# Moving the pieces of a later chunk's trunk between the gather steps of the chunk before it

## The chip, the cores and the metric

The kernel runs on one core of one Trainium2 chip. A time is the device's time for one execution, in microseconds (us); three runs of the kernel before gave a median of 3059.66 us (3058.35 to 3059.75). One further execution was recorded by the profiler, and all rows below are from it. The engines are TensorE (PE, matmuls, and PEld for its weight loads), VectorE (DVE), ScalarE (ACT), GpSimd (POOL) and SyncE (SP), which only asks for DMA transfers here.

## The reference

One layer of a decoder over 1024 prompt tokens and 8 sample tokens of width 1024, in float32:

```
h = rmsnorm(x);  u, x_lru, y_lru, g_a, g_b = split(h @ w_in)
a_out = S5(u): 32 groups, complex state of 64, h_t = a h_{t-1} + B u_t, y = C h + d u,
        z = gelu(y), a_out = z * sigmoid(z @ w_glu + b_glu)
b_out = RG-LRU(conv4(x_lru)) * gelu(y_lru):  r, i = sigmoid(block-diagonal gates of xc),
        log_a = -8 r softplus(-lam), h_t = exp(log_a) h_{t-1} + sqrt(1 - exp(2 log_a)) (i * xc)
x = x + (sigmoid(g_a) * (a_out @ w_proj_a) + sigmoid(g_b) * (b_out @ w_proj_b)) @ w_out
# PEER: 8 heads x top 16 of 128 x 128 experts a token
q = rmsnorm(x) @ w_q;  scores of two key halves, top 16 of each, top 16 of the 256 sums
x = x + sum over 128 experts e of  softmax(score)_e * gelu(u_tab[e] . x) * v_tab[e]
y = rmsnorm(x)
```

The outputs are y for both kinds of tokens and the last states of S5, RG-LRU and the convolution.

## The kernel before

**Chunks and steps.** The prompt is cut into CH = 4 chunks of C = 256 tokens. What stands ahead of PEER (in-projection, convolution, S5, RG-LRU, GLU, mixing, output, queries and lists of experts) is called a chunk's trunk. PEER then takes, for each of a chunk's two tiles of 128 tokens, 128 experts a token: one indirect DMA by POOL (`gather`, L802) brings for 128 tokens the row of u and the row of v of one expert each, 128 x 8 KB = 1.05 MB. There are 1032 of them in all. Two gathers are one step (PAIR = 2) and a chunk has BC = 128 steps. For each gather DVE does one dot product over 1024 elements (L1825, with a read-out of its sum), ACT weighs it (L856), and PE does eight matmuls on v (`values`, L2273, of the step before).

**What lets a gather go.** The u rows stand in a ring of CHAINS = 5, the v rows in a ring of UV = 10. POOL's gather i waits until the dot product of gather i-5 is done (`u_used`), and until the matmuls of gather i-10 are. So the order of work on DVE decides when POOL may ask for the next rows: a DVE that waits for something else holds the gathers.

**The calendar.** The trunk of chunk c (1 to 3) runs between the last steps of chunk c-1. Each engine has its own program, written out in order; before a piece of the trunk it calls `upto(t)`, which first lets the engine do its part of the gather steps up to calendar time t. A time t up to 96 is a step of chunk c-1: step 48 + 80t/96 (rounded down) for chunk 1, step 32 + t for chunks 2 and 3; from 96 on it is a step of the chunk itself. The functions `at_...` (from L126) give the times. Nothing but semaphores ties the engines to each other: where the calendars of a maker and of a user of data give the same step, the user waits for the maker with its own gather work still to do behind the wait.

**The pieces that the change touches.** On DVE a later chunk's list is `LATER_DVE`, "CCCC--" + "SSSS" + "LLS" four times + 16 "S": piece n stands at `at_piece(n)`. C is a convolution, L a piece of the RG-LRU recurrence (`lru`, L1315 and L1620; the first L of a chunk waits for `tanh_ok`, which ACT's square root gives), S a piece of S5 (`s5`, L1307, L1582), three to each of 8 pairs of state rows. The first piece of a pair waits for `bu_ok`: PE's `s5_in` (L2178, 16 matmuls of 32 x 128) at `at_s5_in(jp)`. The first `s5_in` also waits for ACT, which must have copied the inputs u out of PE's banks. Then come PE's gate units (`project`, L2161, at `at_ga`), the four GLU units (L2161; ACT; then DVE's L1315, four of 128 x 256), the eight mixing units (`mix`: L2317 on PE at `at_mix(m)`, three L1315 on DVE at `at_mix(m)` + 1) and the eight output units (`out`, L2337, at `at_out(k)`).

**Weights.** SP brings a pair of weight tiles of 1 MB (w_in, L678), or 512 KB (w_glu, w_ab), when the slot of an earlier pair comes free.

```
def at_s5_in(jp):
    return max(at_scan(PIECES * jp) - 2, 9)
def steps_at(c, t):
    old = BC - own(c - 1) if c else OLD
    return t * old // OLD if t <= OLD else old + t - OLD
```

Of the kernel before, what the change touches and what calls it, by code (L numbers as in the profile page):

```python
# [72 lines left out]
LAST_FIRST = (6, 7, 0, 1, 2, 3, 4, 5)  # L73


AT_GATE, AT_GA, AT_GLU, AT_MIX, AT_OUT, AT_X2, AT_TR, AT_PROJ, AT_Q = 8, 24, 51, 53, 62, 71, 74, 75, 81
SECOND_AT = 10

TRUNK_W = [("w_in", m) for m in range(28)] + [("w_glu", m) for m in range(4)]
# [44 lines left out]


def at_piece(n):  # L126
    return 3 + 6 * n // 5


def at_scan(k):  # L130

    return at_piece([n for n, kind in enumerate(LATER_DVE) if kind == "S"][k])
# [30 lines left out]

def at_ga(m):

    return AT_GA + 25 * m // 16


def later_u(q):
# [10 lines left out]


def at_mix(m):
    return AT_MIX + m


def at_out(k):
    return AT_OUT + 9 * k // 8


def at_proj(h, s):  # L190
# [201 lines left out]
def build(nc, i_, o_):  # L392

    with ExitStack() as ctx:
# [459 lines left out]
        def _(act):  # L854
# [224 lines left out]
            def chunk(c, last):  # L1079
# [95 lines left out]
                else:  # L1175
# [32 lines left out]
                    for m in range(2 * KT):  # L1208
                        z_until(at_ga(m) + 1)
                        upto(at_ga(m) + 1)  # L1210
                        mixing_gate(m)
# [91 lines left out]
        def _(dve):  # L1303
# [724 lines left out]
            def chunk(c, last):  # L2028
# [13 lines left out]
                for n_piece, kind in enumerate(FIRST_DVE if first else LATER_DVE):  # L2042
                    upto(at_piece(n_piece))
                    if kind == "S":
                        next(scans)
                    elif kind == "L":
                        next(gates)
                    elif kind == "C" and not first:
                        conv(c, convs, last)
                        convs += 1  # L2050
                        if convs == QT:
                            if last:
                                V.tensor_copy(hsmp, xl[:, :, 3 + C:3 + N])
                            V.tensor_copy(halo, xl[:, :, C:C + 3]).then_inc(halo_ok, 1)
# [9 lines left out]
                for m in range(KT):  # L2064
                    upto(at_mix(m) + 1)
                    mix(c, m, units(c) + U_MIX + m, slice(0, n), MIXB[m % 2])
# [59 lines left out]
        def _(pe):  # L2126
# [348 lines left out]
            def chunk(c, last):  # L2475
# [48 lines left out]
                else:  # L2524
# [12 lines left out]
                    for m in range(2 * KT):  # L2537
                        due_at(at_ga(m))
                        project(c, ga_unit(c, m), U_GATE + m, hT[c], KT, n)
# [18 lines left out]
                for m in range(KT):  # L2558
                    upto(at_mix(m))
                    if m == 0:  # L2560
                        pe.wait_ge(lru_ok, QT * (c + 1))
                        pe.wait_ge(a_ok, QT * (c + 1))
                    if m >= 2:
                        pe.wait_ge(mix_ok, mixes(c) + m - 1)
                    mix(c, 32 + m, MIXB[m % 2], slice(0, n))
                for k in range(KT):
                    upto(at_out(k))
                    if k == 0:
                        pe.wait_ge(evac, evacs(c) + U_MIX)
                        pe.wait_ge(mix_ok, mixes(c + 1))  # L2570
                        pe.wait_ge(yo_ok, 2 * c - 1)
                    out(c, 40 + k, k, rows_of(last))
# [138 lines left out]
```

## Time and profile before

| | |
|---|---|
| median of three runs | 3059.66 us (3058.35 to 3059.75) |
| profiled execution | 3058.84 us, span 3057.0 us |
| busy share | PE 80%, DVE 71%, ACT 39%, POOL 37% |
| granted TensorE clock, mean | 0.875 of full speed |
| DMA | 1215.48 MB, mean 398 GB/s |
| of these the gathers | 1082.20 MB, 85.7% of the DMA engines' span |
| weights and the like (SP) | 126.19 MB, 10.4% |

A busy share is a mean over the span. The page also cuts the span into 40 slices of 76 us and gives the bytes a second of each. In a timeline row the columns are the start, the duration, engine, line, operation, tiles, shapes and count; the bracket at the end gives the idle time of the engine just before it and what ended it. In a row of windows a stretch is followed by its length and by the busy time of each engine.

### The profile page before, as it was taken

How to read it: one execution, taken by the hardware profiler on the slowest of the kernel's cores; microseconds unless marked ns; L12 is line 12 of the kernel's file. 1: busy time of each engine (PE TensorE's matmuls, PEld its weight loads, DVE VectorE, ACT ScalarE, POOL GpSimd, SP SyncE). 2: the span in 40 equal slices, each digit the busy share in tenths (PEclk: the TensorE clock that was granted, in tenths of full speed). 3: DMA queues.
4: the chain of work that ended last, by engine and by line, in shares of the span. 5: the costliest groups of instructions: out<-in, count | busy, mean ns of one | idle time of the engine just before them, and what ended most of it. 6: DMA issues, size and time to landing. Idle time of an engine off the chain costs nothing.

```text
span 3057.0 us, 43457 instructions
## 1 busy us (share of the span) xinstructions
PE 2434.5 (80%) x14644; PEld 1174.7 (38%) x14644; DVE 2163.9 (71%) x5371; ACT 1204.7 (39%) x3783; POOL 1122.0 (37%) x1048
## 2 busy tenths in 40 slices
PE   9997768898887778898877778888987766766676
PEld 7864324555343324455333324454433321111111
DVE  7757887776479886676468987676558897554445
ACT  2224444433344444333335444433244444333333
POOL 0014443333334443333334444333334444433332
PEclk9998888999988889999978878999989896676677
DMA  4569999999999999999999999999999999999998
GB/s 155 199 244 388 414 416 421 417 419 399 411 420 412 416 420 420 421 415 420 420 421 403 410 420 413 421 414 420 419 418 414 408 416 418 420 421 421 420 421 339
DMA packets 176079, 1215.48 MB, mean 398 GB/s; under 512 B 22360, under 2 KB 22744, under 8 KB 31472
## 3 DMA queue, kind: packets, MB, share of 16 engines
q0 software_dynamic: 148608, 1082.20, 85.7%
q1 hardware_dynamic: 25744, 126.19, 10.4%
q10 hardware_dynamic: 1504, 4.33, 0.4%
q8 instruction: 115, 1.88, 0.2%
q14 instruction: 108, 0.88, 0.1%
HBM read 1208.12 MB, written 4.51 MB: 397 GB/s over the span
## 4 chain that ended last, share of the span: by engine, by line
DMA 29%; issue 26%; PE 18%; POOL 12%; DVE 12%; ACT 2%; DVEq 0%; ACTq 0%; POOLq 0%; SPq 0%
DMA arena<-in_uv,arena 16%; POOL arena L802 12%; DMA arena<-in_vu,arena 12%; PE psum L2273 7%; DVE arena L1825 5%; PE psum L2161 4%; DVE arena L1307 3%; PE psum L2317 2%; ACT arena L856 2%; PE psum L2337 1%; DVE arena L1315 1%; PE psum L2349 1%; PE psum L2384 0%; DVE arena L1688 0%; PE psum L2178 0%
## 5 line engine op out<-in xcount | busy, mean ns | idle before, releaser
L1825 DVE CUSTOM_DVE_ANT_0 arena<-arena 128x1024 f32<-128x1024 f32 x1024 | 1247.1, 1225 | 752.3 <-DMA arena<-in_uv,arena 377.0
L2273 PE MATMUL psum<-arena 64*64 64x512 f32 x8184 | 1280.1, 727 | 562.0 <-ACT arena L856 497.7
L856 ACT ACTIVATE arena<-arena 128x1 f32<-128x1 f32 (+3 forms) x3252 | 931.6, 289 | 1626.9 <-DVE arena L1825 1441.2
L802 POOL DMA_INDIRECT arena<-in_vu,arena x517 | 555.1, 1074 | 1007.8 <-DVE arena L1825 708.4
L802 POOL DMA_INDIRECT arena<-in_uv,arena x515 | 563.7, 1095 | 904.7 <-DVE arena L1825 775.6
L2273 PEld LDWEIGHTS psum<-arena 64*64 64x64 f32 x8184 | 276.0, 150 | 1374.0 <-ACT arena L856 1071.2
L2161 PE MATMUL psum<-arena 128*128 128x256 f32 (+1 forms) x2656 | 643.1, 398 | 5.4 <-DVE arena L1315 2.6
L2161 PEld LDWEIGHTS psum<-arena 128*128 128x128 f32 x2656 | 511.1, 197 | 199.6 <-issue 121.2
L1307 DVE TENSOR_TENSOR arena<-arena 128x256 f32<-128x256 f32 (+11 forms) x562 | 250.1, 471 | 12.9 <-ACT psum L856 0.8
L856 ACT ACT_TABLE_LOAD x119 | 152.7, 1283 | 11.0 <-DVE arena L1307 7.0
L856 ACT ACTIVATE arena<-psum 128x256 f32<-128x256 f32 (+5 forms) x254 | 98.9, 402 | 120.8 <-PE psum L2161 80.8
L2317 PE MATMUL psum<-arena 128*128 128x128 f32 (+2 forms) x640 | 119.0, 342 | 6.4 <-DMA arena<-in_w_ab 4.2
L2317 PEld LDWEIGHTS psum<-arena 128*128 128x128 f32 x640 | 100.0, 190 | 32.8 <-issue 17.1
L1315 DVE SCALAR_TENSOR_TENSOR arena<-arena 128x256 f32<-128x256 f32 (+8 forms) x287 | 97.9, 354 | 20.6 <-ACT arena L856 15.3
L2337 PE MATMUL psum<-arena 128*128 128x512 f32 x192 | 91.3, 619 | 0.0
L1825 DVE DVE_READ_ACCUMULATOR2_ANT arena<- 128x1 f32 x1024 | 84.7, 83 | 0.0
L1315 DVE SCALAR_TENSOR_TENSOR arena<-arena,psum 128x128 f32<-128x128 f32 (+5 forms) x102 | 52.5, 551 | 28.3 <-PE psum L2317 24.0
L1582 DVE TENSOR_TENSOR_SCAN arena<-arena 128x64 f32<-128x64 f32 x256 | 68.9, 332 | 1.4
L2349 PE MATMUL psum<-arena 128*128 128x256 f32 (+1 forms) x320 | 62.3, 350 | 0.4 <-issue 0.4
L1307 DVE TENSOR_TENSOR arena<-psum,arena 128x512 f32<-128x512 f32 (+2 forms) x91 | 59.7, 685 | 2.7 <-PE psum L2178 1.0
L2349 PEld LDWEIGHTS psum<-arena 128*128 128x128 f32 x320 | 51.8, 196 | 22.7 <-issue 18.0
L2337 PEld LDWEIGHTS psum<-arena 128*128 128x128 f32 x192 | 35.7, 195 | 55.9 <-issue 55.9
(139 smaller groups left out, 1049.2 us busy)
## 6 DMA issues: line engine op xcount, KB each, us to landing
arena<-in_w_in SPq DMA_DIRECT2D x56, 1024.0 KB
arena<-in_w_q SPq DMA_DIRECT2D x34, 1024.0 KB
arena<-in_vu,arena POOLq DMA_INDIRECT x517
arena<-in_uv,arena POOLq DMA_INDIRECT x515
arena<-in_w_ab SPq DMA_DIRECT2D x11, 512.0 KB, 11.1
arena<-in_keys SPq DMA_DIRECT2D x17, 256.0 KB, 8.8
arena<-in_w_out SPq DMA_DIRECT2D x8, 512.0 KB, 16.0
arena<-in_x_tok SPq DMA_DIRECT2D x8, 512.0 KB
```

The source lines that it names most:

```text
L802: pool.indirect_dma_start(rows_[:, first:first + 2 * D], None, table, bass.IndirectOffsetOnAxis(column, 0)).then_inc(uv_in[at % UV], 16)
L856: return nc.scalar.activation(out, in_, f, **kw)
L1307: return V.tensor_tensor(out, a, b, op)
L1315: return V.scalar_tensor_tensor(out=out, in0=a, scalar=s1, in1=b, op0=op0, op1=op1)
L1582: return V.tensor_tensor_scan(v, mag2[:, j:j + 1].to_broadcast([P, SEG]), v, start, ALU.mult, ALU.add)
L1825: V.tensor_tensor_reduce(out=u, in0=u, in1=hn, scale=1.0, scalar=0.0, op0=ALU.mult, op1=ALU.add, accum_out=dots_[:, b % DOTS, k:k + 1]).th ...
L2161: ins = mm(PB[u % 2][:, 0:n], w[:, P * t:P * t + P], rhs[:, t, 0:n], start=(t == 0), stop=(t == k - 1))
L2273: ins = mm(PV[o:o + HP, half], dg[r:r + HP, PAIR * (b % 2) + k], cells[r:r + HP, v_cell(place(c, i)), at:at + 512], start=(i % (SLOT // 2) ...
L2317: ins = mm(banks[side][:, 0:cols.stop - cols.start], w[:, 512 * side + P * t:512 * side + P * t + P], src[:, t, cols], start=(t == 0), sto ...
L2337: ins = mm(OUTB[t][half][0:rn], hT[c][:, k, r0:r0 + rn], w[:, 512 * half:512 * half + 512], start=(k == 0), stop=(k == KT - 1))
L2349: ins = mm(PB[s][:, 0:n], w[:, P * t:P * t + P], gb[:, t, cols], start=(t == 0), stop=(t == KT - 1))
```

## The change

Five constants or slopes of the later chunks' calendar change. The pieces of DVE stand at 3 + 9n/8 where they stood at 3 + 6n/5, and `at_s5_in` follows them, but not below 9; the 16 gate units take 22 calendar steps where they took 25; GLU begins at 48 (was 51), mixing at 50 with 5/4 step a unit (was 53 with one), output at 61 with 5/4 (was 62 with 9/8). The other trunk pieces keep their times. Chunk 0's own trunk is not touched.

```
-AT_GATE, AT_GA, AT_GLU, AT_MIX, AT_OUT, AT_X2, AT_TR, AT_PROJ, AT_Q = 8, 24, 51, 53, 62, 71, 74, 75, 81
+AT_GATE, AT_GA, AT_GLU, AT_MIX, AT_OUT, AT_X2, AT_TR, AT_PROJ, AT_Q = 8, 24, 48, 50, 61, 71, 74, 75, 81
 def at_piece(n):
-    return 3 + 6 * n // 5
+    return 3 + 9 * n // 8
 def at_ga(m):
-    return AT_GA + 25 * m // 16
+    return AT_GA + 22 * m // 16
 def at_mix(m):
-    return AT_MIX + m
+    return AT_MIX + 5 * m // 4
 def at_out(k):
-    return AT_OUT + 9 * k // 8
+    return AT_OUT + 5 * k // 4
```

DVE, where chunk 1's first S5 piece (L1307 from PE's bank `psum`) stands among the dot products of chunk 0 (L1825; four rows are a step), the difference between before (-) and after (+):

```order
 L1825 ISA arena<-arena 128x1024
 L1825 ISA arena 128x1
-L1825 ISA arena<-arena 128x1024
-L1825 ISA arena 128x1
-L1825 ISA arena<-arena 128x1024
-L1825 ISA arena 128x1
 L1307 TENSOR_TENSOR arena<-psum,arena 128x512 x2
 L1307 TENSOR_TENSOR arena<-arena 128x2x128 x2
```

The piece now comes one step earlier. PE's `s5_in` for it stays at calendar time 9, so that both stand at the same step, where DVE's stood one later. The same holds in chunks 2 and 3.

DVE again, chunk 1's first recurrence piece (the last row) after the piece that begins S5's second pair, before:

```order
 L1307 TENSOR_TENSOR arena<-psum,arena 128x512 x2
 L1307 TENSOR_TENSOR arena<-arena 128x2x128 x2
 L1825 ISA arena<-arena 128x1024
 L1825 ISA arena 128x1
 L1825 ISA arena<-arena 128x1024
 L1825 ISA arena 128x1
 L1825 ISA arena<-arena 128x1024
 L1825 ISA arena 128x1
 L1825 ISA arena<-arena 128x1024
 L1825 ISA arena 128x1
 L1315 SCALAR_TENSOR_TENSOR arena<-arena 128x256 x2
```

and after:

```order
 L1307 TENSOR_TENSOR arena<-psum,arena 128x512 x2
 L1307 TENSOR_TENSOR arena<-arena 128x2x128 x2
 L1825 ISA arena<-arena 128x1024
 L1825 ISA arena 128x1
 L1825 ISA arena<-arena 128x1024
 L1825 ISA arena 128x1
 L1315 SCALAR_TENSOR_TENSOR arena<-arena 128x256 x2
```

It has come one step nearer; ACT's work for it has not moved.

PE, chunk 1's GLU (L2161 x16, four units of four) and mixing (L2317; eight are a unit) among the values of chunk 0 (L2273; eight are a step), before:

```order
 L2161 MATMUL psum<-arena 128x256 x16
 L2273 MATMUL psum<-arena 64x512 x16
 L2317 MATMUL psum<-arena 128x256 x8
 L2273 MATMUL psum<-arena 64x512 x8
 L2239 MATMUL psum<-arena 128x128 x8
 L2317 MATMUL psum<-arena 128x256 x16
 L2273 MATMUL psum<-arena 64x512 x8
 L2317 MATMUL psum<-arena 128x256 x8
 L2273 MATMUL psum<-arena 64x512 x8
```

and after:

```order
 L2161 MATMUL psum<-arena 128x256 x16
 L2273 MATMUL psum<-arena 64x512 x8
 L2317 MATMUL psum<-arena 128x256 x8
 L2273 MATMUL psum<-arena 64x512 x8
 L2317 MATMUL psum<-arena 128x256 x8
 L2273 MATMUL psum<-arena 64x512 x8
 L2317 MATMUL psum<-arena 128x256 x8
 L2273 MATMUL psum<-arena 64x512 x8
 L2317 MATMUL psum<-arena 128x256 x8
 L2273 MATMUL psum<-arena 64x512 x8
 L2239 MATMUL psum<-arena 128x128 x8
 L2317 MATMUL psum<-arena 128x256 x8
```

Two mixing units stood in one step before; after, each has a step of its own. In chunk 1 the compressed calendar puts DVE's half of GLU at the same step (40 steps of chunk 0 after its step 48) as PE's half; before it stood one step later. In chunks 2 and 3 it stays one step later.

## Rows read from the trace of the kernel before

**Rows 1.** The page's part 2: GB/s moved in 40 equal slices of the span.

```profile
GB/s 155 199 244 388 414 416 421 417 419 399 411 420 412 416 420 420 421 415 420 420 421 403 410 420 413 421 414 420 419 418 414 408 416 418 420 421 421 420 421 339
```

**Rows 2.** Windows: stretch, us, busy of PE, PEld, DVE, ACT, POOL; PEclk, DMA share, GB/s.

```profile
676.00:692.00 16.00, 16.00 (x124) 11.11 (x123) 12.96 (x33) 5.44 (x19) 5.02 (x6) 1.00 1.01 419
740.00:755.00 15.00, 15.00 (x84) 10.39 (x83) 11.81 (x23) 5.08 (x18) 7.38 (x6) 1.00 0.82 310
770.00:785.00 15.00, 15.00 (x75) 5.99 (x74) 6.91 (x13) 4.23 (x15) 6.47 (x5) 1.00 0.97 372
1303.00:1315.00 12.00, 9.92 (x66) 5.91 (x66) 11.68 (x30) 7.73 (x19) 5.23 (x4) 1.00 0.96 388
513.00:521.00 8.00, 6.62 (x38) 3.25 (x40) 2.54 (x7) 2.44 (x7) 2.09 (x3) 0.54 1.02 423
```

**Rows 3.** Timeline: gathers that POOL issued late, a weight pair, a mixing unit's wait.

```profile
672.20 0.33 SPq L678 DMA_DIRECT2D arena<-in_w_in  x1
683.61 0.94 POOL L802 DMA_INDIRECT arena<-in_vu,arena  x1 [5.20 <-DVE arena L1825]
740.90 0.75 DVE L1315 SCALAR_TENSOR_TENSOR arena<-arena,psum 128x256 f32<-128x256 f32 x2 [3.91 <-PE psum L2317]
744.92 1.68 POOL L802 DMA_INDIRECT arena<-in_vu,arena  x1 [7.84 <-DVE arena L1825]
1307.43 1.68 POOL L802 DMA_INDIRECT arena<-in_vu,arena  x1 [4.72 <-DVE arena L1825]
```

**Rows 4.** Timeline around chunk 1's first S5 piece.

```profile
509.26 0.33 SPq L678 DMA_DIRECT2D arena<-in_w_in  x1
511.80 1.23 DVE L1825 CUSTOM_DVE_ANT_0 arena<-arena 128x1024 f32<-128x1024 f32 x1 [1.25 <-DMA arena<-in_uv,arena]
513.60 0.94 POOL L802 DMA_INDIRECT arena<-in_vu,arena  x1 [1.83 <-DVE arena L1825]
515.28 3.62 PE L2273 MATMUL psum<-arena 64*64 64x512 f32 x14
518.84 2.08 PE L2178 MATMUL psum<-arena 32*128 32x128 f32 x16
522.97 1.22 DVE L1825 CUSTOM_DVE_ANT_0 arena<-arena 128x1024 f32<-128x1024 f32 x1
```

**Rows 5.** Timeline: the same place in chunks 2 and 3.

```profile
1163.98 0.94 POOL L802 DMA_INDIRECT arena<-in_vu,arena  x1 [1.53 <-DVE arena L1825]
1169.26 1.16 PE L2178 MATMUL psum<-arena 32*128 32x128 f32 x16
...
1882.04 0.94 POOL L802 DMA_INDIRECT arena<-in_uv,arena  x1 [1.54 <-DVE arena L1825]
1887.66 2.08 PE L2178 MATMUL psum<-arena 32*128 32x128 f32 x16
```

**Rows 6.** Timeline: the first recurrence piece's root in chunk 1, then chunk 2.

```profile
536.64 1.22 DVE L1825 CUSTOM_DVE_ANT_0 arena<-arena 128x1024 f32<-128x1024 f32 x1
538.63 0.33 SPq L678 DMA_DIRECT2D arena<-in_w_in  x1
543.87 1.06 ACT L856 ACTIVATE arena<-arena 128x1024 f32<-128x1024 f32 x1
...
1189.80 1.23 DVE L1825 CUSTOM_DVE_ANT_0 arena<-arena 128x1024 f32<-128x1024 f32 x1 [0.60 <-DMA arena<-in_uv,arena]
1195.53 1.06 ACT L856 ACTIVATE arena<-arena 128x1024 f32<-128x1024 f32 x1
```

**Rows 7.** Timeline around chunk 1's GLU.

```profile
701.80 1.95 PE L2273 MATMUL psum<-arena 64*64 64x512 f32 x16
707.11 0.94 POOL L802 DMA_INDIRECT arena<-in_vu,arena  x1 [0.30 <-issue]
715.25 4.61 PE L2161 MATMUL psum<-arena 128*128 128x256 f32 x13
724.50 0.43 DVE L1315 SCALAR_TENSOR_TENSOR arena<-arena 128x256 f32<-128x256 f32 x1 [1.24 <-ACT arena L856]
```

## The prediction

> **What bounds the kernel now.** I read the page's slices first. From the fourth on, the DMA engines move 388 to 421 GB/s in every slice but the last, and 420 or 421 is the ceiling at which the row stops again and again [rows 1]. The gathers carry 1082 of 1215 MB, and the change adds and removes no byte. So the later 2.7 ms are a transfer at its full rate with small holes, and an edit is worth what it does to those holes: a microsecond in which the queue of gathers runs dry is not given back later, since everything behind it is at the ceiling too. PE is busy 80% of the span and DVE 71%, yet a wait on either costs nothing as long as enough gathers are under way.
>
> Next I looked for the holes, with windows around gathers that POOL issued late. Rows 3 give the idle time G of POOL ahead of an issue (always ended by a dot product), rows 2 the rate around it. The loss in a window is its length times (1 - rate/421).
>
> - G = 7.84 at 744.92: 740 to 755 ran at 310, a loss of 15 x (1 - 310/421) = 3.95 us.
> - G = 4.72 at 1307.43: 1303 to 1315 at 388, a loss of 0.94.
> - G = 5.20 at 683.61: 676 to 692 at 419, a loss of 0.1, though G is longer than in the case above. There SP had asked for a weight pair at 672.20; ahead of the two others no pair stands.
>
> So the loss is G less a cover. The cover is what still stands in the queue at the last issue: 7.84 - 3.95 = 3.9 and 4.72 - 0.94 = 3.8 without a pair; with one, 1.05 MB at 421 GB/s is 2.5 us more, hence 6.3, which the third case allows (it shows only that the cover is at least 5.1). The sum below is made with 3.8 and 6.3.
>
> **The change part by part.** All of it is a shift of work on PE, ACT and DVE against the gather steps; no operation is added, so no duration is new. What is new is where a user now stands at its maker's step.
>
> *The first S5 piece of each later chunk.* DVE's piece moves one step earlier, PE's `s5_in` does not. Behind DVE's wait stand its next dot products, and behind those POOL's gathers. In chunk 1 [rows 4]: the last dot product ahead of the piece is the one at 511.80, which ends at 513.03; its gather is issued 0.57 us later and POOL is done at 514.54. `s5_in` is done at 518.84 + 2.08 = 520.92. From there to the end of the first dot product behind the piece took 522.97 + 1.22 - 520.92 = 3.27 us before, and would again; with the 0.57 the next gather goes at 524.76. G = 10.2; a weight pair was asked for at 509.26, 4.3 us ahead of the last issue, so the cover is 6.3 and the loss 3.9. DVE itself waits 520.92 - 513.1 = 7.8 us.
>
> In chunks 2 and 3 [rows 5] the same sum gives G = 1169.26 + 1.16 + 3.27 + 0.57 - (1163.98 + 0.94) = 9.3, loss 3.0, and G = 1887.66 + 2.08 + 3.84 - (1882.04 + 0.94) = 10.6, loss 4.3. The pairs of these chunks are asked for at the same calendar time as in chunk 1, since SP's order follows the trunk units, which do not move here. Together 11.2 us; without the pairs' cover it would be 2.5 more for each.
>
> *The first recurrence piece.* It waits for ACT's root, whose place is fixed, and comes one step earlier. Chunk 1 [rows 6]: the last dot product ahead of it now is that of 536.64, ending 537.86, its gather's issue done at 537.86 + 0.57 + 0.94 = 539.4; the root is done at 544.93; the piece (0.7), a dot product (1.2) and 0.57 later the next gather goes, at 547.4: G = 8.0, a pair was asked for at 538.63, loss 1.7. Chunk 2: the dot product ends 1191.03, the issue 1192.5, the root 1196.59, the next issue 1199.1: G = 6.6, loss 0.3 if a pair covers it, 2.8 if not. I take 0.3, as chunk 1 has its pair at this place, and as much for chunk 3. Together 2.3, at most 7.3.
>
> *Chunk 1's GLU.* PE's half moves from step 90 of chunk 0 to step 88, DVE's from 91 to 88, so that DVE now waits for all of it. In the times of before PE would begin at 703.75, behind the values of 701.80; from PE's first GLU matmul at 715.25 to DVE's last piece at 724.50 + 0.43 it took 9.7 us [rows 7]. So DVE goes on at 713.4, POOL at 715.2, with its last issue done at 707.11 + 0.94 = 708.05: G = 7.2, loss 0.9 with a full pair in the queue, 3.4 with none. I take the middle, 2.1, as the tiles of this stage are half as large.
>
> *Mixing.* Chunk 1's two mixing units in one step made DVE wait 3.91 us for PE [rows 3]; each has its own step after the change, and with it go the loss of 3.95 in 740 to 755 and that of 770 to 785 at 372 GB/s, 15 x (1 - 372/421) = 1.75 [rows 2]. Gain 5.7. It cannot be more, as those windows then run at 421; if the second hole is of the next stage, it is 3.95. In chunks 2 and 3 a unit already has a step of its own, so 5/4 steps give nothing there. What is late next there is again the gather, 2.5 us for each at 421 GB/s.
>
> A sentence of the Trainium skill bears on how this hole is read. The busy share of the DMA engines in 770 to 785 is 0.97 while the rate is 372 [rows 2]. The page Perfetto Trace Analysis, section Identifying the Most-Contended Engine, has one judge DMA by how much of the memory's bandwidth is used and not by occupancy, since 16 engines make the latter misleading. By occupancy the two windows would give 15 x 0.18 + 15 x 0.03 = 3.2 us and the sum would be 2.5 worse; by rate 5.7. The row sides with the page: 0.97 and 1.01 stand beside rates 12% apart.
>
> *The rest.* Output units, gate units and the later S5 pieces move by one to four steps and keep at least one step between maker and user. Their cover is the dot product's own wait for its gather (1.25 us at 511.80), in which DVE has time to spare. I take 0; if the denser gate units hold PE up it is a loss of 2, if spreading output helps a gain of 1.
>
> Sum: 11.2 + 2.3 + 2.1 - 5.7 = +9.9 us on the profiled 3058.84 us, so 3068.7, say 3069. The median of before lies 0.8 us above the profiled run, too little to correct for.
>
> **The rivals.**
>
> *The queue hides every wait, and only the gain remains (not slower).* Up to five gathers of 2.5 us are out at once, 12.5 us, and a pair on top. From a cover of 10.6 us on, each G above is hidden: 3058.8 - 5.7 = 3053.1. For it: the pairs are asked for only some 4 us before the last issue in the S5 places, against 11.4 us at 683.61, so more of them still stands in the queue. Against it: at 744.92 five places were allowed as well, and all but 3.9 us of the wait was lost.
>
> *The cover with a pair is a microsecond longer than 6.3*, for the same reason. Then S5 loses 2.9 + 2.0 + 3.3 = 8.2, the recurrence 0.7, GLU 0.9, and the sum is 9.8 - 5.7 = +4.1: 3063.
>
> *PE falls to half clock behind the new waits.* From 513 to 521 the granted clock was 0.54, close to the lower of the two levels (1.2 GHz of 2.4) [rows 2], and there 14 value matmuls took 3.62 us [rows 4] where 16 take 1.95 at full clock [rows 7]; `s5_in` took 2.08 against 1.16 in chunk 2 [rows 5]. That much is already in the sum. If PE, now short of dot products for 8 us more, is slow for the second S5 pair as well, that piece waits by some 2.2 + 0.9 us in each chunk, 3 x 3 = 9 more: 3078. For it: the row of 513 to 521. Against it: the second pair keeps a step between maker and user. The Trainium skill's page TensorE: Matmul & The Clock Gate, section HAM oscillation, describes such kernels: each wait drops the clock to half and the next burst starts cold; by that rule the last time holds, and no run here yet shows it for the second pair.
>
> **How the numbers follow.** The forecast has a chance of 0.50, with a range of its own of 3065 to 3073; the full hiding 0.13, the longer cover 0.27, the clock 0.10. A measurement of this kernel can tell about 0.2%, 6.1 us, from no change, so slower means above 3065.8 and faster below 3053.5. Slower: nine tenths of the forecast, a fifth of the longer cover and all of the clock case, 0.45 + 0.05 + 0.10 = 0.60. Faster: half of the full hiding, 0.06. The same: the remaining 0.34. The range of 3056 to 3076 leaves out most of the full hiding and of the clock case.
>
> **What would show it.** In the profile after, DVE's row of the first S5 piece (L1307, 128x512) should show a wait of 7 to 8 us for PE L2178 in each of the three later chunks, POOL a gather behind it with 9 to 11 us of idle time, and the windows there a rate of 300 to 340 GB/s over some 15 us, where 423 stands now. The recurrence piece in chunk 1 should wait about 7 us for ACT. The rate between 740 and 785 should be about 420. The prediction is wrong if the POOL gaps are there and the rate stays at 420 (cover), if the waits are not there (the lead is not what I read), or if the holes lie elsewhere.

## The result and the profile after

The changed kernel takes 3072.43 us (median of 7 runs, 3066.17 to 3078.67) against 3059.44 us of the kernel before on the same chips: a ratio of 1.004 (1.0031 to 1.005), 13.0 us more, where 9.9 was forecast. The profiled execution took 3072.93 us with a span of 3071.1 us. Its page moves the same bytes; a few slices that stood at 412 to 420 now stand at 387 to 408:

```profile
GB/s 155 203 243 382 414 413 409 416 420 396 420 421 408 416 418 395 421 399 421 420 420 413 415 419 387 420 408 420 419 418 417 410 414 418 418 421 421 421 421 341
```

To say where, I cut each trace at the dot products of every eighth step, and took from each stretch's length its bytes divided by 421.8 GB/s, the rate that I take for the ceiling (full windows show 419 to 424). What is left is transfer time lost. Summed over four kinds of stretches (us; an estimate worked out from all DMA records of one profiled execution each, most of the start of the execution left out):

| lost in | steps | before | before, second look | changed |
|---|---|---|---|---|
| first S5 piece | chunk 0: 48-56; 1 and 2: 40-48 | 0.4 | 0.4 | 9.9 |
| chunk 1's recurrence | chunk 0: 56-64 | 0.8 | 0.3 | 2.0 |
| chunk 1's GLU, mixing | chunk 0: 80-104 | 5.9 | 5.4 | 4.9 |
| fifth S5 pair, norm of the second tile | chunks 1 and 2: 64-72 | 2.3 | 3.0 | 6.6 |
| everything else | | 39.9 | 41.6 | 39.9 |
| sum | | 49.3 | 50.7 | 63.4 |

(The first line holds chunk 2's and chunk 3's first recurrence piece as well, which lie in the same stretches.) The four places take up 14.0 of the 14.1 us by which the spans differ; against the second look they take 14.3 of 12.7, so "everything else" is uncertain by some 2 us.

**First S5 piece.** The timeline after, at the places of [rows 4, 5], chunk 1, then 2, then 3:

```profile
519.98 1.16 PE L2178 MATMUL psum<-arena 32*128 32x128 f32 x16
521.18 1.29 DVE L1307 TENSOR_TENSOR arena<-psum,arena 128x512 f32<-128x512 f32 x2 [6.24 <-PE psum L2178]
524.68 1.68 POOL L802 DMA_INDIRECT arena<-in_uv,arena  x1 [8.23 <-DVE arena L1825]
...
1174.07 1.35 PE L2178 MATMUL psum<-arena 32*128 32x128 f32 x16
1175.47 1.29 DVE L1307 TENSOR_TENSOR arena<-psum,arena 128x512 f32<-128x512 f32 x2 [7.20 <-PE psum L2178]
1178.97 1.68 POOL L802 DMA_INDIRECT arena<-in_vu,arena  x1 [9.49 <-DVE arena L1825]
...
1899.27 1.29 DVE L1307 TENSOR_TENSOR arena<-psum,arena 128x512 f32<-128x512 f32 x2 [7.13 <-PE psum L2178]
1903.06 1.39 POOL L802 DMA_INDIRECT arena<-in_uv,arena  x1 [9.71 <-DVE arena L1825]
```

DVE waits for PE's `s5_in`, then POOL has been idle for 8 to 10 us. Windows of the stretches right behind them (columns as in [rows 2]; in [rows 2] the stretch 513 to 521 stood at 423):

```profile
529.00:537.00 8.00, 7.31 (x44) 4.59 (x41) 7.90 (x18) 5.44 (x18) 5.55 (x4) 1.00 0.97 363
1180.00:1192.00 12.00, 11.27 (x88) 5.54 (x80) 10.49 (x28) 7.65 (x25) 7.86 (x7) 1.00 0.85 297
1903.00:1915.00 12.00, 10.72 (x80) 5.51 (x84) 11.17 (x30) 7.92 (x26) 8.69 (x6) 1.00 0.85 291
```

**The first recurrence piece**, chunk 1, at the place of [rows 6]:

```profile
546.14 0.76 DVE L1315 SCALAR_TENSOR_TENSOR arena<-arena 128x256 f32<-128x256 f32 x2 [6.75 <-ACT arena L856]
548.32 1.68 POOL L802 DMA_INDIRECT arena<-in_vu,arena  x1 [6.87 <-DVE arena L1825]
```

**GLU and mixing of chunk 1**, at the places of [rows 7] and [rows 3]:

```profile
712.84 3.78 SPq L678 DMA_DIRECT2D arena<-in_w_ab  x2
718.65 1.68 POOL L802 DMA_INDIRECT arena<-in_vu,arena  x1 [7.50 <-DVE arena L1825]
720.73 5.27 PE L2317 MATMUL psum<-arena 128*128 128x256 f32 x16 [2.59 <-DMA arena<-in_w_ab]
726.04 0.75 DVE L1315 SCALAR_TENSOR_TENSOR arena<-arena,psum 128x256 f32<-128x256 f32 x2 [4.22 <-PE psum L2317]
...
742.63 0.75 DVE L1315 SCALAR_TENSOR_TENSOR arena<-arena,psum 128x256 f32<-128x256 f32 x2 [2.03 <-PE psum L2317]
744.40 2.05 PE L2239 MATMUL psum<-arena 128*128 128x128 f32 x16
746.58 1.28 DVE L1315 SCALAR_TENSOR_TENSOR arena<-arena,psum 128x1024 f32<-128x1024 f32 x1 [2.66 <-PE psum L2239]
749.27 1.68 POOL L802 DMA_INDIRECT arena<-in_vu,arena  x1 [6.62 <-DVE arena L1825]
```

```profile
718.00:748.00 30.00, 27.41 (x156) 18.43 (x153) 16.98 (x35) 8.47 (x30) 13.27 (x10) 0.94 1.01 419
748.00:754.00 6.00, 6.00 (x36) 3.87 (x35) 5.53 (x11) 2.88 (x11) 4.12 (x3) 1.00 0.47 130
```

The hole of [rows 2] at 770 to 785 is gone:

```profile
770.00:785.00 15.00, 15.00 (x64) 5.54 (x64) 4.96 (x10) 4.24 (x15) 6.53 (x6) 1.00 1.02 419
```

That of 740 to 755 is not: it stands at 748 to 754, at 130 GB/s. GLU's wait (POOL idle 7.50) costs nothing where it stands, since 718 to 748 runs at 419. But behind it DVE waits 4.22 us for the first mixing unit and about 2 us for each of the next ones. I take it that the queue therefore doesn't fill again, and that the broadcast of the finished tile's output norm (PE's L2239 at step 92, then DVE's product of 128x1024 at step 93, in both kernels) meets it empty; the 130 GB/s fit that.

**The fifth S5 pair.** A wait that I had not forecast, in chunk 1's step 63:

```profile
1305.25 3.78 PE L2239 MATMUL psum<-arena 128*128 128x128 f32 x16 [6.54 <-DVE arena L1307]
1309.14 1.28 DVE L1315 SCALAR_TENSOR_TENSOR arena<-arena,psum 128x1024 f32<-128x1024 f32 x1 [3.15 <-issue]
1312.41 1.39 POOL L802 DMA_INDIRECT arena<-in_uv,arena  x1 [7.21 <-DVE arena L1825]
```

```profile
1312.00:1327.00 15.00, 15.00 (x115) 9.42 (x114) 14.64 (x37) 9.58 (x26) 7.57 (x6) 1.00 0.82 308
```

At step 63 PE broadcasts a norm's weights (L2239) with which DVE makes the inputs of the chunk's second tile at step 64. (It is the norm ahead of PEER; the expectations below call it the output norm.) The broadcast overwrites the bank from which DVE reads S5's input products, so by the program it waits until DVE has read every pair whose `s5_in` comes earlier. Before, these were four pairs; with the denser pieces the fifth pair's `s5_in` moves from step 64 to 62 and its DVE piece from 66 to 64, right ahead of the product. PE waits 6.54 us for DVE, and then DVE waits 3.15 us for PE (its releaser isn't in the row; the product reads what L2239 writes).

### The profile page after: what moved, and what is told of

Same layout as the page of the kernel before. It is cut to its first block, busy times and chain, and to the rows that moved or that the text cites. A ratio compares the mean times of both kernels' runs of the same rounds, so it can differ in the third digit from the quotient of the medians.

```text
span 3071.1 us, 43457 instructions
## 1 busy us (share of the span) xinstructions
PE 2449.3 (80%) x14644; PEld 1180.1 (38%) x14644; DVE 2161.8 (70%) x5371; ACT 1207.2 (39%) x3783; POOL 1134.7 (37%) x1048
## 4 chain that ended last, share of the span: by engine, by line
DMA 30%; PE 27%; issue 16%; DVE 14%; POOL 8%; ACT 4%; DVEq 0%; ACTq 0%; POOLq 0%
DMA arena<-in_uv,arena 15%; DMA arena<-in_vu,arena 14%; PE psum L2273 10%; POOL arena L802 8%; PE psum L2161 8%; DVE arena L1825 6%; PE psum L2317 3%; DVE arena L1307 3%; ACT arena L856 3%; DVE arena L1315 1%; PE psum L2337 1%; PE psum L2349 1%; ACT L856 1%; DMA arena<-in_w_ab 1%; PE psum L2239 1%
## 5 line engine op out<-in xcount | busy, mean ns | idle before, releaser
L1825 DVE CUSTOM_DVE_ANT_0 arena<-arena 128x1024 f32<-128x1024 f32 x1024 | 1244.9, 1225 | 721.1 <-DMA arena<-in_uv,arena 338.1
L2273 PE MATMUL psum<-arena 64*64 64x512 f32 x8184 | 1282.8, 730 | 556.6 <-ACT arena L856 483.2
L802 POOL DMA_INDIRECT arena<-in_vu,arena x517 | 561.8, 1087 | 1003.1 <-DVE arena L1825 676.5
L2273 PEld LDWEIGHTS psum<-arena 64*64 64x64 f32 x8184 | 273.4, 150 | 1383.5 <-ACT arena L856 1017.7
L2161 PE MATMUL psum<-arena 128*128 128x256 f32 (+1 forms) x2656 | 647.3, 400 | 3.0 <-DVE arena L1315 1.9
L2161 PEld LDWEIGHTS psum<-arena 128*128 128x128 f32 x2656 | 514.7, 199 | 188.7 <-issue 109.9
L1307 DVE TENSOR_TENSOR arena<-arena 128x256 f32<-128x256 f32 (+11 forms) x562 | 250.3, 472 | 12.9 <-ACT psum L856 0.8
L2317 PE MATMUL psum<-arena 128*128 128x128 f32 (+2 forms) x640 | 120.9, 345 | 6.9 <-DMA arena<-in_w_ab 4.6
L2317 PEld LDWEIGHTS psum<-arena 128*128 128x128 f32 x640 | 101.0, 192 | 34.4 <-issue 18.4
L1825 DVE DVE_READ_ACCUMULATOR2_ANT arena<- 128x1 f32 x1024 | 84.6, 83 | 0.0
L1307 DVE TENSOR_TENSOR arena<-psum,arena 128x512 f32<-128x512 f32 (+2 forms) x91 | 59.7, 686 | 22.3 <-PE psum L2178 20.6
L2337 PEld LDWEIGHTS psum<-arena 128*128 128x128 f32 x192 | 36.1, 198 | 57.8 <-issue 57.8
```

The source lines that it names most:

```text
L802: pool.indirect_dma_start(rows_[:, first:first + 2 * D], None, table, bass.IndirectOffsetOnAxis(column, 0)).then_inc(uv_in[at % UV], 16)
L1307: return V.tensor_tensor(out, a, b, op)
L1825: V.tensor_tensor_reduce(out=u, in0=u, in1=hn, scale=1.0, scalar=0.0, op0=ALU.mult, op1=ALU.add, accum_out=dots_[:, b % DOTS, k:k + 1]).th ...
L2161: ins = mm(PB[u % 2][:, 0:n], w[:, P * t:P * t + P], rhs[:, t, 0:n], start=(t == 0), stop=(t == k - 1))
L2273: ins = mm(PV[o:o + HP, half], dg[r:r + HP, PAIR * (b % 2) + k], cells[r:r + HP, v_cell(place(c, i)), at:at + 512], start=(i % (SLOT // 2) ...
L2317: ins = mm(banks[side][:, 0:cols.stop - cols.start], w[:, 512 * side + P * t:512 * side + P * t + P], src[:, t, cols], start=(t == 0), sto ...
```

## The experiments

Each run stands beside runs of the kernel before on the same chip. The lost time by the places of the table above, of one profiled execution each, in the same order:

| run | us, median | ratio to before | S5 | recurrence | GLU, mixing | fifth pair | else |
|---|---|---|---|---|---|---|---|
| changed | 3072.43 | 1.004 (1.0031 to 1.005) | 9.9 | 2.0 | 4.9 | 6.6 | 39.9 |
| a1_first_s5_back | 3062.42 | 1.0006 (0.9997 to 1.0015) | 1.3 | 0.8 | 6.9 | 5.0 | 39.6 |
| a2_first_s5_alone | 3062.96 | 1.0013 (1.0004 to 1.0022) | 7.5 | 2.1 | 5.9 | 1.6 | 36.1 |
| a3_mix_alone | 3056.78 | 0.9992 (0.9983 to 1.0001) | 0.4 | 0.2 | 0.5 | 2.6 | 42.5 |
| a4_fifth_pair_back | 3071.95 | 1.0035 (1.0023 to 1.0047) | 9.3 | 2.3 | 7.9 | 7.9 | 38.1 |
| c1_glu_mix_later | 3067.99 | 1.0029 (1.002 to 1.0037) | 10.3 | 1.8 | 0.6 | 6.9 | 39.9 |
| c2_first_s5_glu_mix | 3060.39 | 1.0005 (0.9996 to 1.0013) | 0.9 | 3.3 | 0.8 | 10.3 | 37.6 |
| d1_fifth_pair_alone | 3064.49 | 1.0017 (1.0009 to 1.0026) | 0.4 | 0.2 | 5.8 | 9.3 | 42.6 |
| e1_mix_and_gates | 3057.53 | 0.9995 (0.9987 to 1.0004) | 0.4 | 0.2 | 1.4 | 4.9 | 38.5 |
| e2_mix_and_s5 | 3056.11 | 0.9991 (0.9982 to 1.0) | 0.6 | 0.2 | 0.5 | 1.4 | 42.9 |
| e3_first_s5_and_recurrence | 3066.79 | 1.0023 (1.0012 to 1.0034) | 8.0 | 1.9 | 4.6 | 1.3 | 38.4 |
| e4_cured_recurrence_back | 3059.37 | 1.0011 (0.9995 to 1.0026) | 0.4 | 0.2 | 0.7 | 8.0 | 39.6 |

The median of before was 3059.67 for the runs a, 3058.64 for c and d, 3059.11 for e. The column "else" shows what such a sum can tell: it differs by some 3 us to either side between kernels, and so a time is read from the medians, the places from the table. The kernels with these waits also scatter more from run to run (the changed one over 12.5 us in 7 runs, the kernel before over 5.7 in the 28 beside the runs a), so differences of 4 us between two of them are often not clear of noise.

**The first S5 piece, undone and alone.** a1 is the changed kernel, a2 the kernel before:

```
 a1  return 3 + 9 * n // 8 + (1 if n in (6, 7) else 0)
 a2  return 3 + 6 * n // 5 - (1 if n == 6 else 0)
```

> The changed kernel, with the first two S5 pieces of each later chunk one calendar step later (at 10 and 11, as in the kernel before), all else changed. Theory (DVE standing at the step of its maker holds the gathers, and what the queue doesn't cover is lost for good): the three waits of 6 to 7 us for PE L2178 go, and with them a loss of 1.2 + 4.4 + 3.4 = 9 us; 3072.4 - 9 = 3063. Rival (the queue and the weight transfers hide these waits and the loss has another cause): 3070 to 3074. Rival of a half: the wait moves to the next pair, 3068.

> The kernel before, with the first S5 piece of each later chunk one calendar step earlier and nothing else. Theory: three waits of 6 to 8 us for PE L2178, POOL idle 9 to 11 us behind each, and the time grows by 9 to 11 us: 3059.4 + 10 = 3069. Rival (hidden): 3059.

Undone (the first two pieces, 6 and 7), it gave 10.0 us back, as the theory had it. In a1's chunk 2 the piece waits for nothing and the rate stays up:

```profile
1173.38 1.28 DVE L1307 TENSOR_TENSOR arena<-psum,arena 128x512 f32<-128x512 f32 x2
1174.03 0.94 POOL L802 DMA_INDIRECT arena<-in_vu,arena  x1 [2.47 <-DVE arena L1825]
```

```profile
1176.00:1188.00 12.00, 12.00 (x95) 6.91 (x88) 10.96 (x29) 7.22 (x23) 5.18 (x5) 1.00 1.02 419
```

Alone (a2), the waits and the hole are there as forecast:

```profile
1172.87 1.29 DVE L1307 TENSOR_TENSOR arena<-psum,arena 128x512 f32<-128x512 f32 x2 [7.34 <-PE psum L2178]
1176.36 1.68 POOL L802 DMA_INDIRECT arena<-in_vu,arena  x1 [9.63 <-DVE arena L1825]
```

```profile
1176.00:1188.00 12.00, 11.18 (x88) 6.07 (x88) 11.65 (x31) 7.77 (x25) 8.27 (x6) 1.00 0.80 282
```

but the time grew by 3.3 us only, not 10: a miss. The places don't show why: in the columns S5 and recurrence together a2 loses 8.5 us more than before, and undoing saved 9.8, nearly as much. The rest lies in "else", which is lowest in a2. e3 tries one explanation.

**Mixing alone**, on the kernel before:

```
+MIX_PE, MIX_DVE = (53, 54, 56, 57, 58, 59, 60, 62), (54, 56, 57, 58, 59, 60, 62, 63)
-    return AT_MIX + m
+    return MIX_PE[m]
-    return AT_OUT + 9 * k // 8
+    return 64 + 7 * k // 8
-                    upto(at_mix(m) + 1)
+                    upto(MIX_DVE[m])
```

> The kernel before, with the mixing units alone moved so that each has a step of its own in chunk 1 too (PE at 53, 54, 56, 57, 58, 59, 60, 62, DVE a step behind it; output at 64 + 7k/8); GLU, gate units and pieces as before. Theory (the double unit made the two holes of 740 to 785): 4 to 5.7 us less, 3054 to 3055.5. Rival (the first hole comes of GLU and the mixing weights and stays): 1.5 less, 3058. Rival (it is the later output that counts): 3060 or more.

The two holes are filled (5.9 to 0.5 in the table), the time falls by 2.9 us, less than the 4 to 5.7 of the theory; the interval of the ratio just includes 1. The window over both holes:

```profile
731.00:785.00 54.00, 54.00 (x302) 32.38 (x300) 34.78 (x66) 16.46 (x59) 18.92 (x20) 1.00 1.01 420
```

**GLU and mixing further apart in the changed kernel** (c1), and that with the first S5 piece back (c2, with a1's `at_piece`):

```
+MIX_PE, MIX_DVE = (51, 52, 53, 54, 56, 57, 58, 59), (52, 53, 54, 56, 57, 58, 59, 60)
+    return 62 + 9 * k // 8
-                upto(AT_GLU + 1)
+                upto(AT_GLU + 2)
```

> The changed kernel, with DVE's half of GLU one calendar step later (so that in chunk 1 too it stands a step behind PE's) and the mixing units one to two later (PE at 51, 52, 53, 54, 56 to 59, DVE a step behind; output at 62 + 9k/8), all else changed. Theory (the mixing gain was forecast rightly but eaten by a new hole where GLU, its weights' slots and the first mixing unit now stand within two steps): the loss of 4.9 us in chunk 0's steps 80 to 104 falls to about 1, 3072.4 - 4 = 3068.5. Rival (that loss comes of the denser gate units before GLU): 3072.

> The run above with, besides, the first two S5 pieces of each later chunk one step later (10 and 11). Theory (the two causes are apart and add): 3062.4 - 5 = 3057.5, with about 4 us of loss left at the fifth S5 pair. Rival (undoing both gives no more than undoing the S5 piece alone): 3062.

c1 fell by 4.4 us, and the loss there from 4.9 to 0.6, with the gate units as dense as in the changed kernel: so the denser gates alone don't make the new hole; GLU and mixing that stand too close do. The run moves DVE's GLU, mixing and output together and can't tell which of them it is. By time alone the 4.4 us aren't clear of noise (the two ratio intervals overlap); the trace shows the change at the broadcast, where DVE's product now waits 0.34 us and waited 2.66 before this edit:

```profile
740.11 2.05 PE L2242 MATMUL psum<-arena 128*128 128x128 f32 x16
742.29 1.28 DVE L1318 SCALAR_TENSOR_TENSOR arena<-arena,psum 128x1024 f32<-128x1024 f32 x1 [0.34 <-issue]
744.98 1.68 POOL L805 DMA_INDIRECT arena<-in_vu,arena  x1 [3.03 <-DVE arena L1828]
```

(Lines stand three lower in the kernels that add a list of steps, here and below.) c2, at 3060.39, lies between its theory (3057.5) and its rival (3062): both undone gave back 12.0 us, where one by one they gave 10.0 and 4.4. Its fifth pair loses 10.3 where the theory had left some 4.

**The fifth pair**, moved back in the changed kernel (a4) and brought into the kernel before by itself (d1):

```
 a4  FROM_26 = (34, 35, 36, 37, 38, 38, 40, 41, 41, 42, 43, 44)
     return FROM_26[n - 26] if n >= 26 else 3 + 9 * n // 8
 d1  FROM_22 = (28, 28, 30, 31, 32, 33, 34)
     return FROM_22[n - 22] if 22 <= n < 29 else 3 + 6 * n // 5
```

> The changed kernel, with the S5 pieces from the 27th on up to two steps later, so that the fifth pair's input matmuls come behind the broadcast of the output norm again (step 63 of the chunk before), all else changed. Theory: PE's wait of 6.5 us for DVE's fifth pair ahead of L2239, and DVE's wait of 3.2 us for L2239, go in chunks 2 and 3, and with them 3.0 + 1.2 = 4.2 us: 3068. Rival (these steps' loss has another cause): 3072.

> The kernel before, with the S5 pieces 22 to 28 of a later chunk (28, 28, 30, 31, 32, 33, 34) one to two steps earlier, so that the fifth pair's input matmuls come ahead of the broadcast of the output norm at step 63, and nothing else. Theory (PE waits 6 us for DVE there, then DVE 3 us for PE): 3 to 4 us more, 3063. Rival (these steps lose as much in either order, by another wait in the same place): 3059.5.

d1 costs 5.9 us (3064.49 against 3058.64), and DVE waits at the same row:

```profile
1281.45 1.68 POOL L805 DMA_INDIRECT arena<-in_vu,arena  x1 [7.20 <-DVE arena L1828]
...
1298.23 1.95 PE L2276 MATMUL psum<-arena 64*64 64x512 f32 x16
1300.11 2.05 PE L2242 MATMUL psum<-arena 128*128 128x128 f32 x16
1302.27 1.28 DVE L1318 SCALAR_TENSOR_TENSOR arena<-arena,psum 128x1024 f32<-128x1024 f32 x1 [4.00 <-issue]
1305.54 1.39 POOL L805 DMA_INDIRECT arena<-in_uv,arena  x1 [8.05 <-DVE arena L1828]
```

But this isn't the price of the fifth pair by itself. The edit puts three DVE pieces (21, 22, 23) into step 60, behind which POOL is idle for 7.20 us, three steps ahead of the broadcast. And the theory's first half isn't there: PE goes straight from the values to the broadcast (L2242) without a wait for DVE.

a4 missed: nothing came back. PE no longer waits ahead of the broadcast, but `s5_in` of the fifth pair (its L2181) then stands at the step of DVE's product and waits for it, PE goes on at half clock, and DVE waits for PE's values one step later:

```profile
1308.55 1.69 PE L2181 MATMUL psum<-arena 32*128 32x128 f32 x16 [4.59 <-issue]
1310.17 6.51 PE L2164 MATMUL psum<-arena 128*128 128x256 f32 x16
...
1318.62 2.10 DVE L1310 TENSOR_TENSOR arena<-psum,arena 128x512 f32<-128x512 f32 x3 [6.38 <-PE psum L2276]
1319.48 3.72 PE L2164 MATMUL psum<-arena 128*128 128x256 f32 x16
1322.26 1.68 POOL L805 DMA_INDIRECT arena<-in_vu,arena  x1 [8.81 <-DVE arena L1828]
```

In the kernel before, the fifth pair's `s5_in` stands behind the product too (loss 2.3), but no gate unit stands at its step, 64: the values come first, the gate unit (L2161) after them, and DVE's three sums wait for nothing:

```profile
1300.65 4.40 PE L2161 MATMUL psum<-arena 128*128 128x256 f32 x16
1303.80 2.10 DVE L1307 TENSOR_TENSOR arena<-psum,arena 128x512 f32<-128x512 f32 x3
```

With gates in 22 steps one of them lands on step 64, ahead of the values. e1 asks whether that does it.

**A second look at the kernel before** (b0_before_again; no edit):

> The kernel before once more, for a second profile: how far the lost transfer time of a stretch of eight steps differs between two executions of one kernel. Theory: by under 0.5 us in the stretches named (S5, GLU and mixing, the fifth pair), by up to 1.5 us at the start of chunk 0 and at the borders of chunks.

3060.38 us. The four places differ by 0.6 us at most, the rest by 1.7 in all (first table). Single stretches differ by more than the 0.5 us expected: 0.8 at the fifth pair of chunk 1's steps, 0.5 in mixing.

**Denser gate units** (e1: a3 with `AT_GA + 22 * m // 16`), **one more S5 piece off a full step** (e2: a3 with piece 25 one step earlier), **both early waits** (e3: the kernel before with pieces 6 to 11 at `3 + 9 * n // 8`) and **the recurrence back** (e4: c2 with pieces 10 and 11 one later, too).

> The kernel before with the mixing units of the run on mixing alone and with the 16 gate units in 22 calendar steps in place of 25. Theory (denser gate units alone cost nothing, as PE keeps up with the gathers): the time of mixing alone, 3056.8, within 1.5 us. Rival (they make PE late where the output norm, the fifth S5 pair and the values meet, steps 64 to 72 of chunks 1 and 2, which is why moving the fifth pair back did not help): loss there 6 to 8 us in place of 2.6, 3061 or more.

> A version meant to beat both: mixing alone, and besides S5's piece 25 one step earlier (step 64 in place of 65 in chunks 2 and 3), so that the S5 piece and the sums of the finished tile don't stand in one step of DVE. Theory: the gap of 4.7 us in POOL at step 65 of chunks 1 and 2 shrinks and with it up to 2 us of loss, 3055 to 3056.5. Rival (step 64 has the norm's product and becomes as full): 3057 or more.

> The kernel before with pieces 6 to 11 at the changed calendar (first S5 piece and first recurrence piece both at the step of their makers), nothing else. Theory (the first S5 piece is worth 10 us in the changed kernel and 3.5 alone, because there a second wait follows five steps behind it, before the queue of gathers has filled again): 3066 to 3069. Rival (the second wait is hidden, the difference lies elsewhere): 3062 to 3064.

> The changed kernel with the first two S5 pieces and DVE's GLU and mixing set back as in the run before on both, and the first two recurrence pieces one step later (15 and 16), so that no wait of DVE for ACT's root is left. Theory (with no wait ahead of it the queue covers this one): 3060, no change from 3060.4, within 1 us. Rival (this wait costs by itself what was forecast, 2.3 us): 3058.

e1: 3057.53, within the bound for "free"; the loss at the fifth pair is between the two expectations (4.9, of it 3.7 in chunk 1's steps). The time doesn't show it, but the trace has a4's wait: the gate unit stands ahead of the values, and DVE's three sums wait for them.

```profile
1295.84 5.22 PE L2164 MATMUL psum<-arena 128*128 128x256 f32 x16
1303.01 2.10 DVE L1310 TENSOR_TENSOR arena<-psum,arena 128x512 f32<-128x512 f32 x3 [3.38 <-PE psum L2276]
1306.65 1.68 POOL L805 DMA_INDIRECT arena<-in_vu,arena  x1 [8.01 <-DVE arena L1828]
```

In a3, which lacks only the denser gates, the sums don't wait, and POOL is idle 4.72 us where e1 has 8.01. So the denser gate units make this wait, and a4 traded one wait for another; what it is worth in time is not shown.

e2: 3056.11, as expected; the gap of 4.7 us at step 65 is now 3.43 and the loss there 1.4:

```profile
1303.77 1.68 POOL L805 DMA_INDIRECT arena<-in_vu,arena  x1 [3.43 <-DVE arena L1828]
```

It is the fastest of all, 3.0 us under the kernel before (ratio 0.9991, 0.9982 to 1.0), though not clearly under a3. e3: 3066.79, as its theory had it, 7.7 us more than before, where a2 had 3.3 more. That the second wait counts when it follows the first by five steps is not shown, though: the intervals of the two ratios overlap, a2 has a shorter wait at this place itself (its row first, then e3's), and S5 and recurrence together lose 9.7 us in a2 and 9.9 in e3.

```profile
545.08 0.76 DVE L1315 SCALAR_TENSOR_TENSOR arena<-arena 128x256 f32<-128x256 f32 x2 [2.40 <-ACT arena L856]
...
545.88 0.76 DVE L1315 SCALAR_TENSOR_TENSOR arena<-arena 128x256 f32<-128x256 f32 x2 [6.56 <-ACT arena L856]
```

e3's profiled execution was the fastest of its seven (3064.06), so its row of the table is on the low side. e4: 1.0 us less than c2, with overlapping runs (one of e4's twelve took 3087.07, which lifts its ratio; the medians are 0.3 us apart). Without a wait ahead of it the recurrence's wait is worth between the 0 of the theory and the 2.3 of its rival, and the run can't tell them apart.

## Why the prediction was right, and where it was not

The direction held, and the mechanism for the S5 and recurrence pieces. That the sum came out near (9.9 against 13.0) is partly luck. By the places, S5 and recurrence lost 10.8 us where 13.5 was forecast, GLU with mixing saved 1.0 where 3.6 was forecast, and the fifth pair, priced at nothing, lost 4.2: terms too large made up for a part of two misses of 2.6 and 4.2.

- **First S5 piece, 11.2 us.** Right, slightly high. G was 8.2, 9.5 and 9.7 where 10.2, 9.3 and 10.6 stood in the sum; chunk 1's was shorter mostly since 14 of PE's value matmuls took 2.85 us and not 3.62, and `s5_in` 1.16 and not 2.08 [rows 4]. The loss with cover 6.3 would be 1.9, 3.2 and 3.4 for these; the stretches lost 1.2, 4.7 and 3.7 more than before (the last two with the recurrence). Undone, 10.0 us. What the sum did not see is that the piece alone costs 3.3, though it loses 7 us at its places there too. Where the rest comes back in a2 is not settled; a2's "else" is the lowest of all, at 36.1, in small pieces of about 1 us at most at places that don't touch this change. It goes against the prediction's premise that a lost microsecond is not given back later.
- **First recurrence piece, 2.3 us.** The waits are there (6.75 where about 7 was said). Its price is not settled: by medians against the kernel before, 4.4 us behind the S5 wait (e3 less a2, not clear of noise), about 1 or nothing where that is gone (e4); by the places, chunk 1's stretch lost 1.2 us more than before.
- **Chunk 1's GLU, 2.1 us.** G is 7.5, as worked out (7.2), and it costs nothing on the spot. It seems to cost together with mixing, 30 us later, below.
- **Mixing, a gain of 5.7 us.** This is the step that failed. "With it go the loss of 3.95 in 740 to 755 and that of 770 to 785": only the second went. For the kernel before the cause was read rightly: single units alone (a3) filled both holes, 5.4 us by the places, though the time fell by 2.9 only. What the sum left out is that the same change brings GLU to within one step of mixing in chunk 1: the units that then hold DVE for 2 us each, ahead of the output norm's broadcast at steps 92 and 93, make a hole of their own. With GLU and mixing apart (c1) 4.3 us came back at this place, 4.4 in time.
- **"The rest", 0.** Failed. "Output units, gate units and the later S5 pieces ... keep at least one step between maker and user" counts only data; PE's broadcast reuses the bank of the S5 inputs, and the fifth pair slid past it: 4.2 us more lost at this place. d1's 5.9 us have a crowded step 60 in them. The prediction's aside, 2 us if the denser gate units hold PE up, has its wait in a4 and e1, but no price in time.
- **The rivals.** The full hiding is out: 291 to 363 GB/s behind the waits. The longer cover had 8.2 us for the S5 piece and 4.1 in all; neither a2's 3.3, nor the 10.0 undone, nor 13.0 fits it. The half clock did not show at the second S5 pair: its `s5_in` took 1.16 us in all three chunks, at a granted clock of 1.00 in 521 to 529. It stands in a4's 6.51 us.

By medians, e4, which leaves of the change only the later S5 pieces, the denser gates and the earlier start of GLU and mixing, stands 0.3 us above the kernel before; by the places it loses 5.6 us more at the fifth pair and 5.2 less in mixing. Adding single runs (e3's 7.7 and d1's 5.9) gives 13.6, near the 13.0 measured, but d1 holds a second cause and the parts are not shown to add.

## What to carry to other kernels

Where each engine's order is fixed by a calendar, look for users that land on their maker's step, and for buffers reused there as well as for data: a piece moved by one step can hold a whole queue of transfers. Price such a wait by the idle time of the engine that issues transfers, less what is still in the queue. Whether a wait that is hidden alone is paid when another stands a few steps ahead of it, these runs suggest but don't settle. And a hole that one visible wait precedes may have a second cause in the same step; ask what would be late once the first is gone.

## What the runs showed of the hardware

The DMA engines can look almost fully busy and move less: a share of 0.97 at 363 GB/s in the changed kernel's window of 529 to 537. The deeper holes show in the share (0.85 at 291 to 297 GB/s, 0.47 at 130), but less than in the rate. In a4, behind 4.59 us of PE waiting, the stretch had a granted clock of 0.57, close to the lower of the two levels, and 16 matmuls of 128x256 took 6.51 us where 16 of the same shape took 3.72 in its next step:

```profile
1309.00:1317.00 8.00, 8.00 (x34) 6.07 (x34) 2.04 (x4) 1.98 (x7) 1.87 (x2) 0.57 1.02 424
```
